# Layer norm on VectorE in two-scalar operations one slot sooner, and both spatial products ahead of the last gelu

## The reference, cut to what matters

```
proj = h @ w_in                       # h: 256 x 1024
q, k, v, zg = split(proj)
attn = windowed_gqa(q, k, v, sink)    # 8 heads
u, vg = split(gelu(zg))               # each 256 x 512
vn = layer_norm(vg, ln_g, ln_b)       # (vg - mean) * rstd * g + b, over the 512 columns
z = einsum(w_s, vn) + b_s             # per chunk of 128 rows, 8 groups of 64 columns
gm = u * z
mix = concat(rms_norm(attn), rms_norm(gm))
x = x + gate1 * rms_norm(mix @ w_out)
# then 16 experts, each with three matrices of 1024 x 2816 float32, on 32 rows picked per expert
x = x + gate2 * rms_norm(expert_choice_ffn(modulate(rms_norm(x))))
```

## Time and profile before

| What | us |
|---|---|
| median of three runs | 2297.32 (2292.47 to 2297.46) |
| the profiled execution, its own time | 2298.65 |
| its span, first to last instruction | 2296.8 |
| PE, DVE, ACT, POOL busy | 1800.6, 817.2, 526.1, 93.4 |

### The profile page before, as it was taken

How to read it: one execution, slowest core, us unless ns; L and a number is a source line. 1 busy time by engine, 2 the same in 40 slices (tenths; PEclk the granted TensorE clock), 3 DMA queues, 4 the chain that set the end, 5 groups by cost and what they waited for, 6 DMA issues and landing times.

```text
span 2296.8 us, 28704 instructions
## 1 busy us (share of the span) xinstructions
PE 1800.6 (78%) x12608; PEld 1166.0 (51%) x12608; DVE 817.2 (36%) x1224; ACT 526.1 (23%) x794; POOL 93.4 (4%) x140
## 2 busy tenths in 40 slices
PE   7999999999999999998656656656666665665666
PEld 7898899999888998973111112111211111221211
DVE  5755677757657777751001100100100010010011
ACT  5744433456444334530000000000000000000000
POOL 1200000012100000100000000000000000000000
PEclk9999999999999999999787777778877877877787
DMA  8355566754645775479999999999999999999997
GB/s 261 118 171 176 193 220 221 239 158 147 193 131 191 251 253 182 143 320 421 430 428 430 429 429 428 429 429 429 429 429 429 429 429 429 429 429 429 429 429 312
DMA packets 172077, 739.79 MB, mean 322 GB/s; under 512 B 6785, under 2 KB 133249, under 8 KB 146993
## 3 DMA queue, kind: packets, MB, share of 16 engines
q1 hardware_dynamic: 169600, 731.27, 80.2%
q0 software_dynamic: 2352, 6.69, 0.9%
HBM read 736.88 MB, written 1.05 MB: 321 GB/s over the span
## 4 chain that ended last, share of the span: by engine, by line
DMA 49%; PE 41%; DVE 5%; ACT 2%; issue 2%; POOL 1%; SPq 0%; DVEq 0%; POOLq 0%; ACTq 0%
PE PS L356 40%; DMA WB<-in_w_down 24%; DMA WB<-in_w_up 24%; DVE WL L1665 1%; ACT WH L1138 1%; DVE X L1660 1%; POOL T L2456 1%; DMA S<-in_post_mix_g 1%; DVE S L1660 1%; DMA W<-in_w_gate 0%; PE PS L429 0%; DMA W<-in_w_in 0%; DVE S L1657 0%; DVE CN L1657 0%; DVE S L1737 0%
## 5 line engine op out<-in xcount | busy, mean ns | idle before, releaser
L356 PE MATMUL PS<-WB,XS 128*32 128x352 f32 x3552 | 404.9, 615 | 222.3 <-DMA WB<-in_w_up 164.0
L356 PEld LDWEIGHTS PS<-WB,XS 128*32 128x32 f32 x3552 | 130.9, 137 | 494.9 <-DMA WB<-in_w_up 217.6
L1665 DVE TENSOR_TENSOR WL<-W,WH 128x2048 fp32r<-128x2048 f32 x141 | 323.9, 2297 | 130.8 <-ACT WH L1138 130.8
L1660 DVE SCALAR_TENSOR_TENSOR S<-S,PS 128x352 f32<-128x352 f32 (+1 forms) x110 | 63.4, 588 | 772.6 <-ACT S L1630 748.3
L356 PE MATMUL PS<-HTh,WH 128*128 128x256 f32 x1064 | 307.1, 289 | 9.1 <-DVE HTl L1660 7.2
L1138 ACT ACTIVATE WH<-W 128x2048 fp32r<-128x2048 f32 x141 | 269.3, 1910 | 190.7 <-PE PS L356 184.0
L356 PE MATMUL PS<-HTl,WH 128*128 128x256 f32 x1064 | 302.3, 284 | 0.0
L356 PE MATMUL PS<-HTh,WL 128*128 128x256 f32 x1064 | 302.2, 284 | 0.0
L356 PE MATMUL PS<-WB,S 128*32 128x512 f32 x1056 | 196.7, 683 | 71.9 <-DMA WB<-in_w_down 71.9
L356 PEld LDWEIGHTS PS<-HTh,WH 128*128 128x128 f32 x1064 | 205.3, 193 | 12.7 <-issue 8.1
L356 PEld LDWEIGHTS PS<-HTl,WH 128*128 128x128 f32 x1064 | 205.4, 193 | 0.9
(11 more groups left out here) (276 smaller groups left out, 2115.2 us busy)
## 6 DMA issues: line engine op xcount, KB each, us to landing
WB<-in_w_up SPq DMA_DIRECT2D x62, 2816.0 KB, 36.2
WB<-in_w_gate SPq DMA_DIRECT2D x48, 2816.0 KB, 36.1
WB<-in_w_down SPq DMA_DIRECT2D x47, 2816.0 KB, 36.2
CN<-in_w_gate SPq DMA_DIRECT2D x16, 2816.0 KB, 31.5
CN<-in_w_down SPq DMA_DIRECT2D x16, 2816.0 KB, 35.9
W<-in_w_in SPq DMA_DIRECT2D x31, 1024.0 KB, 5.4
S<-in_w_ada SPq DMA_DIRECT2D x24, 1024.0 KB, 5.3
W<-in_w_gate SPq DMA_DIRECT2D x22, 1024.0 KB, 7.9
```

What stands on the lines that cost most here:

```text
L356: return e.matmul(o, l, r, start=start, stop=stop, skip_group_check=True)
L1660: return e.scalar_tensor_tensor(out=o, in0=a, scalar=s, in1=b, op0=o1, op1=o2)
L1665: e.tensor_tensor(M.WL[i][:, :], M.SLOT[m % NW], M.WH[i][:, :].bitcast(F32), ALU.subtract).then_inc(*up("low", m))
```

## The change

Layer norm no longer uses POOL for its gain and bias. DVE does, for both row tiles, (v - mean) * g with one scalar_tensor_tensor, and then, for both, (that) * rstd + b with another, which signals `vn`. It does so right after `head_step(6)`, ahead of `head_step(7)` and of the next unit's `low`. `gelu_poly("u", 1)` goes behind both `spatial` steps, `spatial(1)` ahead of `gelu_out("u", 1)` and both `gated`. The empty `head_step(9)` goes. On PE the seven filler products ahead of the spatial products go. ACT's and SP's programs are unchanged.

```
@@ PE, second()
         for t in range(2):
-            if t == 0:
-                busy(("sgu",), 7)
             ps = take(("sgu", t))
@@ DVE, layer_norm()
             e.wait_ge(*at("ln_rs"))
             ts(K["rs"], K["rs"], 0.5, None, ALU.mult).then_inc(*step())
-            own()
+            e.wait_ge(*at("ln"))
             for t in range(2):
                 v = M.VG[:, t, :]
-                ts(v, v, K["mv"][:, 2 * t:2 * t + 1], K["rs"][:, t:t + 1], ALU.subtract, ALU.mult).then_inc(*up("ln_c", t))
+                stt(v, v, K["mv"][:, 2 * t:2 * t + 1], M.LN[:, 0, :], ALU.subtract, ALU.mult).then_inc(*step())
+            for t in range(2):
+                v = M.VG[:, t, :]
+                own()
+                stt(v, v, K["rs"][:, t:t + 1], M.LN[:, 1, :], ALU.mult, ALU.add).then_inc(*up("vn", t))
@@ DVE, second()
         layer_norm_head()
         head_step(6)
+        layer_norm()
         head_step(7)
         unit()
         gelu_poly("u", 0)
-        layer_norm()
         gelu_out("u", 0)
         head_step(8)
-        gelu_poly("u", 1)
-        head_step(9)
...
         spatial(0)
+        spatial(1)
+        gelu_poly("u", 1)
         gelu_out("u", 1)
         gated(0)
-        spatial(1)
         gated(1)
@@ POOL
     power(K["rs"], K["ms"], 2).then_inc(*up("ln_rs"))
-    e.wait_ge(*at("ln"))
-    for t in range(2):
-        v = M.VG[:, t, :]
-        e.wait_ge(*at("ln_c", t))
-        e.tensor_tensor(v, v, M.LN[:, 0, :], ALU.mult).then_inc(*up("ln_g", t))
-        e.wait_ge(*at("ln_g", t))
-        e.tensor_tensor(v, v, M.LN[:, 1, :], ALU.add).then_inc(*up("vn", t))
```

## The result

The changed kernel takes 2299.69 us (median of 17 runs, 2296.94 to 2301.78), the kernel before 2295.01 (17 runs, 2291.38 to 2297.46). The ratio is 1.0022, 95% interval 1.0015 to 1.0029: slower by 0.22%, or about 5 us (3.4 to 6.7), and inside the 0.3% that the prediction took as no change. The forecast was 2300.2 and +2.9 us on the profiled execution.

What follows compares the result with a forecast made beforehand. Full DMA engines bound the end, their stream's start hanging on the out_units and PE's order; 2298.65 plus 2.9 is 2301.55, less 1.33 gives 2300.2 us, range 2293.0 to 2303.0, forecast as no change within 0.3%.

Steps and rivals of the forecast that it cites:

- PE's own order is the path, ACT second, DVE third: Ahead of the first out_unit: PE's transposes 2.36 us late; without that, ACT would let MXh begin 1.66 us sooner; DVE third.
- The rule of exchange: Out_units to the end: what the first out_unit's start moves, the end of the kernel moves, one for one.
- DVE's balance of nothing: DVE up to the sum of squares: added and saved time sum to -0.3 us, 976.5 to 976.85 against 976.78.
- the waits for tanh: DVE ahead of each gelu_out of u: 0.69 us idle each, for u 1 in place of 0.90.
- The condition that the prediction set on moving `spatial(1)`: DVE's order: moving spatial(1) ahead costs nothing unless spatial 1's products are late on PE.
- The clock stays at 1.2 GHz without the wide fillers: PE from the spatial products on: narrow products do not restore the clock; +2.4 to +3.4 us, chance 0.59.
- The Trainium skill's sentence: PE's clock follows how busy PE is; read literally it is back at 968, the gain case, -1.7 us, chance 0.24.
- The signs: In the changed profile: `vn` by 962.5, transposes at 984.6 to 985.6, first out_unit at 988 to 989, clock 0.50 until 981 or later.
- The size: Whole change: +2.9 us on the profiled execution, the middle of +2.4 to +3.4.
- the branch priced at +3.4: PE's clock does not come back from 966.74 on; transposes at 985.6, 3.4 us late.
- the branch priced at +2.4: PE's clock recovers, then falls again while PE idles for turned(7) around 969.5; transposes at 984.65, 2.4 us late.
- The forecast time: Median of the changed kernel: 2300.2 us, from 2301.55 for the profiled execution and a median 1.33 under it.

Runs made afterwards that it cites:

- e2: Kernel before with only the seven fillers ahead of the spatial products taken out: ratio 1.0028 to before, stretch 30.80 us.
- f2: Only the early layer norm on DVE, fillers and the other steps as in the kernel before: ratio 0.9996 to before, stretch 24.21 us.
- f1: Changed kernel with seven 256-column fillers in PE's idle time ahead of values(2), none ahead of the spatial products: ratio 1.0001 to before, stretch 22.67 us.
- e1: Changed kernel with the seven 256-column fillers put back ahead of the spatial products: ratio 1.0003 to before, stretch 24.88 us.
- e3: Changed kernel with nine 64-column fillers ahead of the spatial products: ratio 1.0029 to before, stretch 31.36 us.
- e5: Changed kernel without the six fillers ahead of the gated rows' transposes: ratio 1.0004 to before, stretch 24.69 us.
- f3_again: Repeat of the changed kernel with fillers in the idle time and every other wait of the stretch filled: 2293.85 us, ratio 0.9999 to before.
- b_again: The kernel before run once more unchanged, for its profile alone: stretch 24.24 us.
- f1_again: Repeat of the changed kernel with seven fillers in PE's idle time ahead of values(2): median 2295.51 us, ratio 1.0007 to before.

## Why the prediction was right

- *PE's own order is the path, ACT second, DVE third*: right. Fillers in or out move the end by themselves (e2), layer norm by itself does not (f2), and after the change PE comes 3.8 us after its data. With PE early (f1), MXh starts directly behind ACT's scaling of `at`.
- *The rule of exchange*: right, the rest is 1309.7 to 1312.2 over fourteen profiles while the first out_unit moves by 11.6.
- *DVE's balance of nothing*: right in its terms: four operations 2.86 us for 2.9, the waits for tanh 0.70 and 0.69 for 0.69, factors(7) 0.48 for 0.5. The sum shows only as an estimate (f2, 15.3 us against 15.45), since PE covers it. The condition that the prediction set on moving `spatial(1)`, that PE not be late, was not met: DVE was idle for 3.23 us after the change and PE's transposes for 1.58 in e1. It did not matter after the change because PE was later still.
- *The clock stays at 1.2 GHz without the wide fillers*: right, in both branches that were named. The transition came behind the idle time in one profile and at the wait for turned(7) in the other.
- *The Trainium skill's sentence* ("TensorE: Matmul & The Clock Gate", Part 1: The HAM clock gate), that the clock follows how busy the engine has been, does not hold here read as busy time: 18.00 of 18 us busy at 0.50 in e3. The measurement decides.
- *The signs*: counted from the last u product they came as forecast. Moved by the 3.68 us that this execution was ahead, `vn` is there at 962.5 (by 962.5), the transposes start at 985.8 (984.6 to 985.6) and the first out_unit at 989.2 (988 to 989). As read off the profile, without that, the out_unit did not move at all.
- *The size*, +2.9 with +2.4 to +3.4: too small. It was +3.62 and +4.10 in the stretches of the two profiles (27.86 and 28.34 against 24.24), and 5 in the runs, whose interval, 3.4 to 6.7, takes in both. In the first profile, the branch priced at +3.4, the six fillers took 4.90; they had been priced at their 4.4 us of before, which had the clock back for their last part. In the second, the branch priced at +2.4, spatial 1 starts 9.50 us after the last u product and not 8.72: the prediction let turned(7) through a little early and charged it 0.45 us, its time at 1.00, where at the fallen clock it takes 0.91. Its six fillers took 5.26. So this branch is no cheaper than the other.
- *The forecast time* was nearer (2300.2 to 2299.69) than the forecast difference, and that is luck: it was hung on a median of three runs, 2297.32, that was 2.3 us above the median of seventeen, which made up for a difference that was about 2 too small.

## What to carry to other kernels

Before a filler product is deleted as waste, look at the granted clock ahead of it and behind it: it may be what brings the clock back. Then its width counts, and not only how long it lasts (e1 against e3), and so does its place: the same seven fillers gave a stretch of 24.88 ahead of the spatial products and of 22.67 in the idle time in front. A filler also costs time, and more of it at the low clock (the six ahead of the gated rows took 2.84 us in e1 and 4.90 to 5.26 in the changed kernel): look whether it covers a wait (e5). A stage of narrow products is best entered with the clock up, since this narrow work did not raise the clock in 18 us, though the shorter stretch was not seen in the times until every wait was filled, and even then not clear of noise against before. And when one event's time drifts by more than the effect between two executions of the same code, cut both profiles at an event just ahead of the change and just behind it, and compare the stretch, not the span.

## What the runs showed of the hardware that was not expected

A PE that is busy without a gap stayed at 1.2 GHz for 18 us under products of 64 and 16 columns and a few transposes (e3: 18.00 of 18 busy, clock 0.50). In each profile with a low stretch behind the last u product the clock came back while 256-column fillers ran or right behind them (before, after, e1, e2, e3, f1, f2 and the repeats; in e5 with transposes just ahead of them), 1.3 to 5.5 us after the first of them; in f3_again it came back under the out_unit's 512-column products. It also fell with no idle time at all, just behind lc, in before, b_again, f1 and f1_again, but not in e1 and f2. What decides between these the runs do not show.

And the same code reached the same instruction of the second block between 957.6 and 961.3 us in different executions, with a short low stretch upstream in one and not in another (from 620 to 630 the clock averages 0.66 in the profile before and 1.00 in the one after); that alone is as large as the change's effect.
